# Running the first blocks of four FFNs and two MLPs chunk by chunk, and moving modulation work and the squares' sums in a weight-streaming fp32 kernel

## The reference, cut to what matters

```python
def swiglu(h, w13, w2):
    gate, up = jnp.split(h @ w13, 2, axis=-1)
    return (jax.nn.silu(gate) * up) @ w2
...
        x = x + 0.5 * swiglu(rms_norm(x, ffn1_norm[l]), ffn1_w13[l], ffn1_w2[l])
...
        x = x + 0.5 * swiglu(rms_norm(x, ffn2_norm[l]), ffn2_w13[l], ffn2_w2[l])
...
        mod = (sc @ w_mod[l] + b_mod[l])[:, None, :]
        sh1, sc1, g1, sh2, sc2, g2 = jnp.split(mod, N_MOD, axis=-1)
        u = modulate(rms_norm_2(h, norm1_g[l]), sh1, sc1)
...
    h = h + g1 * y
    h = h + g2 * sq_relu_mlp(modulate(rms_norm_2(h, norm2_g[l]), sh2, sc2), w_mlp1[l], w_mlp2[l])
```

## Time and profile before

| | |
|---|---|
| median of three runs | 1675.48 us (1673.72 to 1679.06) |
| the profiled execution | 1675.48 us, its span 1673.7 us |
| TensorE busy | 1589.7 us (95%) |
| VectorE busy | 1187.2 us (71%) |
| ScalarE busy | 784.4 us (47%) |
| GpSimd busy | 47.0 us (3%) |
| read from memory | 308.52 MB, 185 GB/s over the span |

### The profile page before, as it was taken

How to read it: one execution, slowest core, us unless ns; L and a number is a source line. 1 busy time by engine, 2 the same in 40 slices (tenths; PEclk the granted TensorE clock), 3 DMA queues, 4 the chain that set the end, 5 groups by cost and what they waited for, 6 DMA issues and landing times.

```text
span 1673.7 us, 30196 instructions
## 1 busy us (share of the span) xinstructions
PE 1589.7 (95%) x12406; PEld 1524.1 (91%) x12406; DVE 1187.2 (71%) x1630; ACT 784.4 (47%) x1121; POOL 47.0 (3%) x46
## 2 busy tenths in 40 slices
PE   6999997899999989999899999999899999889999
PEld 6999996799999989999678999997479999889998
DVE  6887688988878677778767777762677555575564
ACT  5434457634346343445564443441565445354442
POOL 1000010100001010000001000000001000010000
PEclk9999999999999999999999999999799999999999
DMA  6766634366665447566233766630334544235550
GB/s 257 274 236 245 247 151 151 151 229 246 236 229 216 186 165 266 231 235 226 78 125 129 274 252 235 242 142 25 112 120 169 191 176 175 101 126 189 184 179 25
DMA packets 43434, 310.83 MB, mean 186 GB/s; under 512 B 4816, under 2 KB 5072, under 8 KB 6096
## 3 DMA queue, kind: packets, MB, share of 16 engines
q1 hardware_dynamic: 41904, 303.33, 49.0%
q0 software_dynamic: 864, 5.21, 0.9%
q10 hardware_dynamic: 576, 1.05, 0.2%
HBM read 308.52 MB, written 1.05 MB: 185 GB/s over the span
## 4 chain that ended last, share of the span: by engine, by line
PE 69%; DVE 9%; ACT 2%; issue 1%; POOL 0%; POOLq 0%; DVEq 0%; ACTq 0%
PE psum L1482 21%; PE psum L1487 20%; PE psum L1488 20%; DVE w_lo L834 3%; DVE buf L843 1%; ACT w_hi L422 1%; PE psum L1657 1%; PE psum L1555 1%; PE psum L1645 1%; DVE u_lo L934 1%; PE psum L1913 1%; PE psum L1926 1%; DVE x L913 1%; PE psum L1937 0%; PE psum L1756 0%
## 5 line engine op out<-in xcount | busy, mean ns | idle before, releaser
L1482 PE MATMUL psum<-u_hi,w_hi 128*128 128x256 f32 (+2 forms) x2608 | 762.6, 292 | 40.4 <-DVE u_lo L921 14.4
L1487 PE MATMUL psum<-u_lo,w_hi 128*128 128x256 f32 (+2 forms) x2608 | 748.7, 287 | 0.0
L1488 PE MATMUL psum<-u_hi,w_lo 128*128 128x256 f32 (+2 forms) x2608 | 748.3, 287 | 0.0
L834 DVE TENSOR_TENSOR w_lo<-raw,w_hi 128x1024 fp32r<-128x1024 f32 x480 | 565.6, 1223 | 157.6 <-ACT w_hi L422 157.4
L1482 PEld LDWEIGHTS psum<-u_hi,w_hi 128*128 128x128 f32 x2608 | 507.3, 195 | 52.0 <-issue 16.9
L422 ACT ACTIVATE w_hi<-raw 128x1024 fp32r<-128x1024 f32 x480 | 478.2, 1046 | 112.9 <-PE psum L1482 106.0
L1487 PEld LDWEIGHTS psum<-u_lo,w_hi 128*128 128x128 f32 x2608 | 507.5, 195 | 2.1
L1488 PEld LDWEIGHTS psum<-u_hi,w_lo 128*128 128x128 f32 x2608 | 506.7, 194 | 1.3
L1482 PE MATMUL psum<-hid_hi,w_hi 128*128 128x256 f32 x1220 | 346.6, 284 | 7.2 <-DVE hid_lo L1364 4.2
L1487 PE MATMUL psum<-hid_lo,w_hi 128*128 128x256 f32 x1220 | 345.5, 283 | 0.0
L1488 PE MATMUL psum<-hid_hi,w_lo 128*128 128x256 f32 x1220 | 345.4, 283 | 0.0
(11 more groups left out here) (222 smaller groups left out, 942.2 us busy)
## 6 DMA issues: line engine op xcount, KB each, us to landing
...
```

What stands on the lines that cost most here:

```text
L834: ve.tensor_tensor(w_lo[:, u], raw[:, u], w_hi[:, u].bitcast(F32), ALU.subtract).then_inc(S.lo_ready, 1)
L1482: ins = te.matmul(dst, w_hi[:, w], hi, start=first, stop=False, skip_group_check=True)
L1487: te.matmul(dst, w_hi[:, w], lo, start=False, stop=False, skip_group_check=True)
L1488: return te.matmul(dst, w_lo[:, w], hi, start=False, stop=last, skip_group_check=True)
```

## The change

- `by_chunk`, which takes each operand chunk through several units, now serves the first block of each FFN (four units, up(0) and up(1); in ffn0 two, then up(1) alone) and of each MLP (three units, then the fourth alone). The norm's sum (`norm_sum`) comes behind it and goes to bank 0, so that down(0) waits for its reading.
- In the FFNs down runs two steps behind up (`LAG = 2`), with bank 7 for up(2) and four buffers for `hid`. VectorE and ScalarE split units up to number 7 of a stage before `rms`, before it up to 3.
- VectorE adds the squares (`add_squares`), in pieces between the operands; GpSimd keeps this only for the context's norm.
- Modulation: none in the first six steps of an FFN; 16, 16, 20, 20 units in the four FFNs and 24 in mlp0, two in each of 12 steps, summed into columns 300 on of the bank of that step's `up`. The two context groups of ffn0 and ffn1 lie at steps 6 to 13, one unit in a step.
- TensorE's loop in the MLPs is written out.

```diff
-MODS_AT = [0, 0] + [2, 1] * 4 + [1] * (FFS - 10)
...
+LAG = 2
+GROUPS = [(0, 0), (0, 1), (0, 4), (0, 5), (0, 2), (0, 3), (0, 6), (0, 7), (0, 8), (0, 9), (0, 10), (0, 11)]
+GROUPS += [(1, _n) for _n in range(12)]
+HOME = {"ffn0": range(0, 4), "ffn1": range(4, 8), "ffn2": range(8, 13), "ffn3": range(13, 18), "mlp0": range(18, 24),
+        "mlp1": range(24, 24)}
...
+MODS_AT = {"ffn0": [0] * 6 + [1] * 16, "ffn1": [0] * 6 + [1] * 16, "ffn2": [0] * 6 + [2] * 4 + [1] * 12,
+           "ffn3": [0] * 6 + [2] * 4 + [1] * 12, "mlp0": [0] * 3 + [2] * 12 + [0], "mlp1": [0] * MLS}
...
+SUM_AT = {"ffn0": [8, 12, 16, 20], "ffn1": [8, 12, 16, 20], "ffn2": [6, 8, 12, 16, 20], "ffn3": [6, 8, 12, 16, 20],
+          "mlp0": [3, 5, 7, 9, 11, 13], "mlp1": []}
...
+    ORDER[_name] = []
+    for _j, _m in enumerate(_mods):
+        ORDER[_name] += [("up", _j)] * 2 + [("mod", _j)] * _m + [("down", _j - _lag)] * (_wide * (_j >= _lag))
+    for _j in range(len(_mods) - _lag, len(_mods)):
+        ORDER[_name] += [("down", _j)] * _wide
...
+        MOD_ACC[_g] = _i % 2 if _name == "mlp0" else int(_i >= len(_groups) - 3)
...
+NORM_BANK = {n: 0 for n in ("start", "wout", "ctx", "wo", "ffn3", "woe", "pool")}
 PE_SUMS = ["ffn3", "mlp0"]
-POOL_SUMS = {n: i for i, n in enumerate(n for n in NORMS if n not in PE_SUMS)}
+POOL_SUMS = {"ctx": 0}
+DVE_SUMS = {n: i for i, n in enumerate(n for n in NORMS if n not in PE_SUMS and n not in POOL_SUMS)}
...
+UP_BANK = [4, 5, 7] + [4 + _j % 2 for _j in range(3, FFS)]
+MOD_COL = 300
...
-                if name not in PE_SUMS:
+                if name in POOL_SUMS:
...
                     hidden(j)
-                    pump_to(c0 + ff_at("down", j + 1) - 1)
+                    pump_to(unit_at(name, "down", j) - 1)
                     if name == "ffn2" and CTX_FROM <= j < CTX_FROM + NC:
                         context_hi(j - CTX_FROM)
                 hidden(FFS - 2)
-                pump_to(c0 + FFU + 3)
...
-            gain_operand("ffn2_0", "wout", early=AT["ffn1"] + 4)
+            gain_operand("ffn2_0", "wout", early=AT["ffn1"] + 8)
...
+            def add_squares(name, b):
+                dve.wait_ge(S.sq_ready, 4 * NRM[name] + b + 1)
+                if b:
+                    a = buf[4][:, half(0)]
+                    link(ve.tensor_tensor(a, a, buf[4][:, half(b)], ALU.add))
+                if b == 3:
+                    ve.tensor_tensor(buf[4][:, 0:T], buf[4][:, 0:T], buf[4][:, T:2 * T], ALU.add).then_inc(S.ssq_ready, 1)
...
+                        add_squares(name, b - 1)
...
-                    pump_to(c0 + ff_at("down", j + 1) - 1)
-                    if j in MOD_READ:
...
+                    pump_to(unit_at(name, "down", j) - 1)
+                    if j in SUM_AT[name]:
+                        read_modulation(HOME[name][SUM_AT[name].index(j)])
...
-            pump_to(ff_at("down", 0) - 1)
+            for b in range(4):
+                add_squares("start", b)
+            pump_to(7)
...
                     mlp_operand("mlp0", "G2", b - 1)
+                    add_squares("woe", b - 1)
...
+            modulation_done("mlp0")
+            scale_gain("H2", 1, 4, "n2_1")
...
+                if name == "ctx":
+                    pe.wait_ge(S.v_out, 1)
+                te.matmul(psum[:, NORM_BANK.get(name, 7), 0:T], ones, buf[4][:, 0:T], start=True, stop=True)\
...
+            def by_chunk(c, op, dsts, done, w=T, shared=True):
...
+                                      k == 0 and (s % 2 == 0 or not shared), k == NC - 1,
+                                      begins=k == (NC - 1 if s else 0))
...
+                c0, h0, groups = AT[name], STEPS[name], HOME[name]
...
-                up(c0 + ff_at("up", 0), 0, 0, 0, h0, name, between=lambda: norm_sum(norm))
-                up(c0 + ff_at("up", 1), 0, 1, 1, h0)
-                pe.wait_ge(S.ms_ready, NRM[norm] + 1)
-                down(0, 0, c0 + ff_at("down", 0), first=True)
...
+                first = [bank2(UP_BANK[j])[:, n, :] for j in range(2) for n in range(2)]
+                if name == "ffn0":
+                    by_chunk(c0, name, first[:2], S.up_ready)
+                    up(c0 + 2, 0, 1, UP_BANK[1], h0)
+                else:
+                    by_chunk(c0, name, first, S.up_ready)
+                norm_sum(norm)
...
+                    up(unit_at(name, "up", j), 0, j, UP_BANK[j], h0)
+                    if j == 2:
+                        pe.wait_ge(S.ms_ready, NRM[norm] + 1)
+                    down(j - 2, (j - 2) % 4, unit_at(name, "down", j - 2), first=j == 2)
...
-                        down(j - 1, 1 - s % 2, c + 3, 2 * i)
...
+                        down(j - 2, s, c + 3, 2 * i)
...
+                down(FFS - 2, (FFS - 2) % 4, end_of(name) - 2)
...
-                up_pair(c0, 0, 0, 0, name, between=lambda: norm_sum(norm))
+                by_chunk(c0, name, [psum[:, 4 + n, 0:TS] for n in range(3)], S.up_ready, TS, False)
+                norm_sum(norm)
+                all_k(c0 + 3, 0, psum[:, 7, 0:TS], w=TS).then_inc(S.up_ready, 1)
                 pe.wait_ge(S.ms_ready, NRM[norm] + 1)
-                up_pair(c0 + 2, 0, 1, 1)
...
+                for j in range(2, MLS):
+                    up_pair(j)
+                    down(j - 1)
+                    if j in SUM_AT[name]:
+                        g = HOME[name][SUM_AT[name].index(j)]
+                        pe.wait_ge(S.up_scaled, h0 + j + 1)
+                        sum_modulation(g, MOD_ACC[g], last_unit(g), bank=4 + 2 * (j % 2), at=MOD_COL)
+                down(MLS - 1, last=True)
```

240 lines of the change are left out of this document (117 added, 123 removed).

## The result

The changed kernel takes 1648.72 us (median of 4 runs, 1648.02 to 1652.43) against 1674.6 us (4 runs) for the kernel before: a ratio of 0.9834, 95% interval 0.9818 to 0.9850. The profiled execution took 1648.02 us, its span 1646.2. The prediction was 1650.

A forecast was written before the change was run, and what follows sets the result against it. TensorE, busy 1589.7 of 1673.7 us, was taken as the bound, with time only in its waits and half-clock matmuls. Terms 22.0 - 1.1 + 0.5 + 4.4 + 1.5 - 0.2 - 1.5 = 25.6 gave 1650; range 1642 to 1664.

The forecast's parts named there:

- FFN starts: Starts of the four FFNs: four units per chunk remove TensorE's chunk waits, leaving 1.3 us before down(0); 22.0 us gained.
- a third of 96 matmuls at half clock: Start of ffn0: assumed share of the first block at half clock; gain 5.9 us, between 0.6 and 8.3.
- Half clock behind those waits: FFN starts: slow matmuls after the wait before down(0); 1.1 us lost, a fifth of 5.2.
- Additions of squares: VectorE's additions fit beside TensorE's block; part of TensorE's waits for GpSimd goes in the recurrent mixer; 0.5 us gained.
- Modulation out of the first steps: FFNs: the 3.0 us of waits for modulation products and one cold stretch of 1.4 go; 4.4 us gained.
- Lag of two: FFN ends: the last hidden gets a unit's cover more, so two waits of 0.75 us go; 1.5 us gained.
- MLP starts: mlp0 and mlp1: time won on chunks is lost to the norm's chain, a 5.2 us wait and cold clock; -0.2 and -1.5.
- The loop written out: TensorE's loop in the MLPs: mlp0's windows show no gap at its turns, so 0 us.
- Modulation in mlp0: mlp0's twelve steps with two units each: VectorE 11.6 to 11.9 us, level with TensorE's 12.0; 0 us in waits.
- The rival of VectorE as the bound: mlp0: VectorE's steps run 0.7 us over, costing 8 us; 1658, or 1662 with worse MLP starts; chance 0.16.

The follow-up runs named there:

- mods_from_step4: Changed kernel with modulation all in the FFNs: none in the first four steps, two units in each of steps 4 to 9, then one; 1682.40 us.
- pool_adds: Changed kernel with all additions of squares on GpSimd again and the blocks kept; 1652.66 us, ratio 0.9865 to the kernel before.
- mlp_unit0_alone: Changed kernel, but in the MLPs unit 0 alone takes the operand by chunks, then the norm's sum, then units 1 to 3; 1645.30 us.
- combined_mlp_block: Changed kernel with the norm's sum earlier in FFN and MLP blocks, and VectorE's two MLP splits moved behind the first hidden chain; 1647.33 us.

## Why the prediction was right, step by step

The measured time is 1.3 us below the forecast. The medians differ by 25.9 us, for which 25.6 were worked out, the profiled spans by 27.5. Part of that closeness is luck, since terms missed in both directions. Step by step:

- *FFN starts, 22.0*: 5.86, 4.70, 5.59 and 5.11 us (ffn0 to ffn3), 21.3. The block's end, the chain of 7.2 us and up(2)'s cover came as worked out; the wait was 0.98 us instead of 1.3. In ffn0 the good fit is luck: a third of 96 matmuls at half clock was a guess (and gives an end at 24.5, not the 24.3 written), while 14 ran at that pace, and a wait of 0.61 us made up part of the difference. What I had not split is by whom it is earned: beside VectorE's additions the blocks bring 14 us, blocks and additions together 22.
- *Half clock behind those waits, 1.1*: wrong, it is 0; the windows behind them are at 1.00. Waits of 0.72 and 0.98 us left the clock up, those of 4.04, 5.1, 5.2 and 6.7 us were followed by half clock. By the Trainium skill, "TensorE: Matmul & The Clock Gate", section "HAM oscillation", these short waits cost nothing more, and here it was right against the one row I put before it (the stretch at 0.50 behind a wait of 1.03 us). But the rows don't bear its rule out everywhere: of the four waits of 2.2 us in mods_from_step4 three were followed by half clock, so at that length the duration alone doesn't decide. What brought half clock at 407 us in the kernel before stays open.
- *Additions of squares, 0.5*: no cost beside the block, as booked; worth 2.5 us at the start of ffn0, nothing where a block has three or four units. The mixer's wait of 0.54 us for GpSimd is gone, as booked. Put at nothing without a look was what the additions do at the other starts: they delay VectorE's last update of `x`, which costs the two waits of 0.8 us at the mixer and k. pool_adds, where GpSimd adds, has neither. So this term is -1.1, not 0.5.
- *Modulation out of the first steps, 4.4*: the waits are gone. But the term names only what was lost before. The new block makes the placing a condition: with the old one the changed kernel is 31 us slower. For a change that had kept the old places the same working would have been some 26 us off.
- *Lag of two, 1.5 at the ends*: both waits are absent, but they stayed absent with a lag of one, so the reason I gave is wrong; which other edit removed them stays open. At the starts the lag carries everything: without it the whole gain is lost and 0.4% more. I had counted its cover, not what it decides.
- *MLP starts, -0.2 and -1.5*: -0.8 and -1.5. The wait of 5.1 us is as worked out, and so is the half clock behind it in mlp1 (3.3 us for 3.5); in mlp0 it lasts 4.8 us, which is where that term missed. mlp_unit0_alone and combined_mlp_block show that these two are what the block costs there. The loop written out was booked at nothing and never run by itself: outside its start mlp1 takes the same to 0.1 us.
- *Modulation in mlp0, 0*: two steps with one sum take 24.01 us, 12.0 each, as worked out. It is 5.3 us longer and the FFNs as much shorter by six sums. The rival of VectorE as the bound is far from its point: three units a step cost nothing.

The terms as they came out, 21.3 - 1.1 + 4.4 + 1.5 - 0.8 - 1.5, are 23.8 of the 27.5 us between the profiled spans (4.4 is as worked out, since only the waits' absence was read). Of the rest 0.9 is a wait for `w_lo` in ffn0 that I had not listed, and 0.7 lies in unchanged stages: k and v took 55.53 us before and 55.20 now, attention 57.49 and 57.13. Some 2 us stay open.
